# Prompt tiles' output projection and logits: from the merge stage into the samples' attention steps

## The reference

```
mod = silu(c) @ w_ada + b_ada            # sh1, sc1, ga1, sh2, sc2, ga2
h = rms_norm(x, g_pre_mix) * (1 + sc1) + sh1
z = h @ w_in                             # q, k, v, u, s
a = rms_norm(attend(q, k, v, lam), g_subln) * (1 - lam_init)
mix = concatenate([a, s_out]) @ w_out    # 1024 x 1024
x = x + ga1 * rms_norm(mix, g_post_mix)
h2 = rms_norm(x, g_pre_ffn) * (1 + sc2) + sh2
f = hier_moe(h2)                         # 4 + 16 logits a token, top 2 of 16 experts
x = x + ga2 * rms_norm(f, g_post_ffn)
```

## Time and profile before

| | us |
|---|---|
| median of 3 runs | 874.96 (874.81 to 875.82) |
| the profiled execution | 875.83 |
| its span | 874.0 |
| TensorE busy | 764.8 (88%) |
| VectorE busy | 370.9 (42%) |
| ScalarE busy | 166.9 (19%) |
| GpSimd busy | 113.1 (13%) |
| granted TensorE clock, mean | 0.942 |
| DMA, mean over the span | 285 GB/s |

### The profile page before, as it was taken

One profiled execution on the slowest core, in us unless ns is written; L12 is line 12 of the kernel. 1 busy time (PEld: TensorE's weight loads), 2 busy tenths in 40 slices (PEclk: granted clock), 3 DMA queues, 4 the chain that ended last, 5 costly groups with the idle time before them and its releaser, 6 DMA issues. The chain is left out here.

```text
span 874.0 us, 12193 instructions
## 1 busy us (share of the span) xinstructions
PE 764.8 (88%) x5016; PEld 366.6 (42%) x5016; DVE 370.9 (42%) x840; ACT 166.9 (19%) x362; POOL 113.1 (13%) x161
## 2 busy tenths in 40 slices
PE   4699999999998486675779996899999999999994
PEld 3144444444444253333434554444444444444431
DVE  2212262447779897677313667410031011100146
ACT  4001000134455112111201221111011110111132
POOL 2220010200002221121200111000000000000054
PEclk9799999999999898778989997799999999999997
DMA  8988194650004969998989715198889999999792
GB/s 312 393 261 363 35 416 169 225 186 13 13 13 153 382 278 424 429 426 378 372 293 299 320 34 218 49 411 325 333 317 408 421 398 417 401 400 405 305 300 110
DMA packets 37146, 249.26 MB, mean 285 GB/s; under 512 B 4809, under 2 KB 6217, under 8 KB 23650
## 3 DMA queue, kind: packets, MB, share of 16 engines
q1 hardware_dynamic: 23490, 156.35, 45.6%
q0 software_dynamic: 9376, 81.47, 23.9%
q10 hardware_dynamic: 4224, 10.65, 3.6%
HBM read 231.92 MB, written 16.53 MB: 284 GB/s over the span
## 5 line engine op out<-in xcount | busy, mean ns | idle before, releaser
L2351 PE MATMUL ps<-sb 128*128 128x512 f32 (+1 forms) x256 | 112.9, 594 | 0.0
L778 PE MATMUL ps<-sb 128*128 128x512 f32 x192 | 87.1, 609 | 1.4 <-DVE sb L436 1.4
L1429 PE MATMUL ps<-sb 128*32 128x256 f32 x512 | 43.6, 501 | 42.8 <-DMA sb<-in_cache_v,ints 39.3
L2275 DVE TENSOR_TENSOR sb<-sb,ps 128x512 f32<-128x512 f32 (+1 forms) x16 | 10.9, 684 | 160.3 <-PE ps L2351 87.1
L817 DVE STREAM_TRANSPOSE sb<-sb 128x1024 f32<-128x1024 f32 (+1 forms) x72 | 75.8, 1097 | 1.1 <-DMA sb<-in_cache_k,ints 1.1
L2341 PE MATMUL ps<-sb 128*128 128x512 f32 x144 | 66.5, 616 | 1.0 <-ACT sb L2193 0.9
L2376 PE MATMUL ps<-sb 128*128 128x512 f32 x144 | 63.5, 594 | 0.0
L1071 PE MATMUL ps<-sb 128*128 128x512 f32 x128 | 59.2, 598 | 0.3 <-DVE sb L974 0.3
L1997 PE MATMUL ps<-sb 128*128 128x512 f32 x128 | 56.7, 596 | 3.1 <-DVE sb L1693 3.1
L2351 PEld LDWEIGHTS ps<-sb 128*128 128x128 f32 (+1 forms) x256 | 42.1, 167 | 33.9 <-issue 33.9
L778 PEld LDWEIGHTS ps<-sb 128*128 128x128 f32 x192 | 36.5, 195 | 45.7 <-issue 44.4
(11 more groups left out here) (349 smaller groups left out, 962.6 us busy)
## 6 DMA issues: line engine op xcount, KB each, us to landing
sb<-in_w_gate SPq DMA_DIRECT2D x16, 2048.0 KB, 18.8
sb<-in_w_up SPq DMA_DIRECT2D x16, 2048.0 KB, 9.9
sb<-in_w_down SPq DMA_DIRECT2D x16, 2048.0 KB, 14.7
sb<-in_w_ada SPq DMA_DIRECT2D x12, 2048.0 KB, 18.5
sb<-in_w_in SPq DMA_DIRECT2D x5, 2048.0 KB, 24.3
y_rows<-sb SPq DMA_DIRECT2D x9, 512.0 KB, 15.2
sb<-in_w_out SPq DMA_DIRECT2D x2, 2048.0 KB, 25.5
sb<-in_x_prompt SPq DMA_DIRECT2D x4, 512.0 KB, 5.0
```

Source lines behind the costliest of these rows:

```text
L778: last = pe.matmul(PS[:, n % 4, :], L.hT[:, k, t * P:t * P + P], w[:, k, :], start=k == 0, stop=k == KC - 1)
L1429: last = pe.matmul(PS[c:c + 32, 7, 0:256], at[:, page, 32 * quad:32 * quad + 32], vp[:, g, 256 * quad:256 * quad + 256], start=page < 2, s ...
L2351: last = pe.matmul(PS[0:n, 1, :], x[:, k, :], w_up[:, k, :], start=k == 0, stop=k == KC - 1)
```

## The change

The prompt tiles' part of merge moves into attend_sample. TensorE's step b becomes: weights of b - 1, scores of b, values of b - 1, then in odd steps up to 5 the transposes of a tile's mix, in even steps the transposes of a tile's x1, then one half of a tile's projection, and in even steps the logits of that tile. Scores have one buffer instead of two; the first mix tile is turned ahead of the first scores, the first half is projected ahead of the weights of sample 0. ACT does all square sums, all copies of turned tiles, of the weights and of the raw logits, and keeps the first half of a projection in SBUF so that one PSUM bank serves both. x is no longer loaded but added by an accumulating DMA of POOL onto the scaled projection. w_out has a place of its own and is fetched at the start of the stage, the second half after the samples' own scores. Logits of prompt tiles are all made from x1 with scaled router weights. merge keeps tile 3's x1 transposes and logits, h2 of all tiles, the samples' tile, and the routing. Buffers move to other places in SBUF.

The core of the diff, TensorE and POOL in attend_sample:

```diff
+            def rows_of(t):
+                pool.wait_ge(sq1, 2 * t + 2)
...
+                pool.tensor_tensor(ss1[:, t:t + 1], ss1[:, t:t + 1], L.cst("half")[:, 0:1], ALU.pow).then_inc(rs1, 1)
+                pool.wait_ge(scaled, 2 * t + 2)
+                pool.dma_start(x1_of(t), a["x_prompt"][0, t * P:(t + 1) * P, :], accum_op=ALU.add).then_inc(x1_in, 16)
...
+                if b % 2 == 0:
+                    rows_of(b // 2 - 1)
                 if b < SB - 2:
                     keys(b + 2)
...
+            def project_half(u):
+                t, c = u // 2, u % 2
+                pe.wait_ge(mix_ev, 2 * t + 2)
+                pe.wait_ge(wo_in[c], 16)
...
+                for k in range(KC):
+                    last = pe.matmul(PS[:, 5, :], mixT(t)[:, k, :], wo[c][:, k, :], start=k == 0, stop=k == KC - 1)
+                last.then_inc(half_done, 1)
...
+            mix_turn(0, 0)
             pe.wait_ge(q_all, 2)
-            for b in range(SB + 1):
+            scores(0, 0)
+            pe.wait_ge(mix_ev, 2)
+            own_scores()
+            project_half(0)
+            for b in range(1, SB + 1):
                 f, par = b - 1, b % 2
+                for part in range(3):
+                    weights(f, part, 1 - par)
                 if b < SB:
                     scores(b, par)
...
+                values(f)
+                if b < SB:
+                    if b % 2 and b <= 5:
+                        mix_turn((b + 1) // 2, b)
+                    if b % 2 == 0:
+                        x1_turn(b // 2 - 1, b)
+                    project_half(b)
+                    if b % 2 == 0:
+                        logits(b // 2 - 1)
```

SP's fetch of w_out, ACT's rows at the start of the stage, and its new place of the x1 square ahead of exp:

```diff
-            sp.wait_ge(s_done, SB)
+            sp.wait_ge(self.grp_done, 5 * NT)
             for c in range(2):
...
+                if c:
+                    sp.wait_ge(own_done, 1)
+                    sp.wait_ge(self.setup, HP + 1)
+                sp.dma_start(wo[c], a["w_out"][0, :, 512 * c:512 * c + 512].rearrange("(p k) n -> p k n", k=KC)
+                             ).then_inc(wo_in[c], 16)
...
+            act.wait_ge(self.v_out, 16 * NT)
...
+            act.dma_start(x1T, a["g_post_mix"].partition_broadcast(P)).then_inc(rows_in, 16)
+            for f in range(2):
+                c = 2 * D + 512 * f
+                act.dma_start(gate[f], self.mod[NS, c:c + 512].partition_broadcast(P)).then_inc(rows_in, 16)
...
+                    if b and b % 2 == 0:
+                        act.wait_ge(x1_in, 16 * t + 16)
+                        if t:
+                            act.wait_ge(log_done, t)
+                        square(x1T, x1_of(t), ss2[:, t:t + 1], sq2)
                     act.wait_ge(m_ready, b + 1)
```

VectorE at step 0 and merge's new order on SP, ACT and VectorE:

```diff
+                if b == 0:
+                    normed(3)
+                    dve.wait_ge(rows_in, 96)
+                    for f in range(2):
+                        last = dve.tensor_tensor(gate[f], gate[f], x1T[:, 512 * f:512 * f + 512], ALU.mult)
...
+            sp.wait_ge(self.sample["pv"], SB - 1)
+            for kind in range(2):
+                self.load_expert(sp, 0, 0, kind)
             sp.wait_ge(self.sample["pv"], SB)
+            self.load_expert(sp, 0, 0, 2)
+            self.load_expert(sp, 1, 1, 0)
+            for i in range(2):
+                sp.wait_ge(h2_out2[i], (48, 32)[i])
             self.load_expert(sp, 1, 1, 1)
             self.load_expert(sp, 1, 1, 2)
...
+            store(1)
+            keep_logits(3)
+            store(2)
+            act.wait_ge(mix_tr, 5)
+            act.activation(mixT, PS[:, 6, :].rearrange("p (k t) -> p k t", k=KC), ACT.Copy).then_inc(mix_ev, 1)
+            store(3)
+            act.wait_ge(summed, 2)
+            square(hv[4][0:NS], proj, ss1[0:NS, 4:5], sq1)
...
+            dve.wait_ge(rows_in, 96 + 16 * 8)
...
+            h2_of(0, scale2, shift2)
+            self.last_sum(SB - 1, 1)
+            h2_of(1, scale2, shift2)
...
+            dve.wait_ge(o_in, 16 * SB)
+            self.head_norm(dve, link, osb, sq, ss8, L.mix[0:NS, 4, 0:512], NS, ss_ready, ss_power, 1
+                           ).then_inc(mix_ready, 1)
             route(0, 3)
+            h2_of(2, scale2, shift2)
+            for c in range(2):
+                dve.wait_ge(half_done, 9 + c)
...
+            h2_of(3, scale2, shift2)
+            dve.wait_ge(rs1, 5)
```

More of the change, by code:

```diff
@@ L1250, in _ @@
[L1250 to L1251 removed]
+                values(b)
+                if b == SB - 2:
+                    pool.wait_ge(s_done, SB - 1)
+                    for half in range(2):
+                        self.load_pages(pool, self.cv, SB - 1, half, LAST_V_SLOT[half])
+                if b % 2 and b >= 3:
+                    t = (b - 3) // 2
+                    pool.wait_ge(sq2, t + 1)
+                    self.power(pool, link, ss2[:, t:t + 1], 1, P, 1.0 / D, rs2)
@@ L1678, in _ @@
+            square(hv[4][0:NS], self.x1[0:NS, 4, :], ss2[0:NS, 4:5], sq2)
+            act.wait_ge(x1_tr, 5)
+            act.activation(h2T, PS[:, 6, :].rearrange("p (k t) -> p k t", k=KC), ACT.Copy).then_inc(x1_ev, 1)
+            store(4)
             act.wait_ge(exp_in, 1)
@@ new lines, in _ @@
+            x1_turn(3, SB)
+            logits(3)
+            pe.wait_ge(mix_ready, 1)
+            pe.wait_ge(self.sample["at_act"], 3 * SB)
+            for k in range(KC):
+                last = pe.transpose(PS[:, 6, NS * k:NS * k + NS], L.mix[0:NS, 4, k::KC], L.cst("ident", NS)[:, 0:NS])
+            last.then_inc(mix_tr, 1)
+            pe.wait_ge(mix_ev, 9)
+            pe.wait_ge(x1_ev, 8)
+            for c in range(2):
+                for k in range(KC // 2):
+                    for c0, kk in ((0, k), (NS, k + KC // 2)):
+                        last = pe.matmul(PS[c0:c0 + NS, 2 + c, :], mixT[:, kk, :], tile["wo"][c][:, kk, :],
+                                         start=k == 0, stop=k == KC // 2 - 1)
+                last.then_inc(half_done, 1)
```

717 lines of the change are left out of this document (305 added, 412 removed).

## The result

The changed kernel takes 909.89 us (median of 4, 907.99 to 912.81), the kernel before 874.88: a ratio of 1.040, interval 1.037 to 1.043. The profiled execution took 909.85 (span 908.0). The forecast was 881, range 862 to 896. The sign was right and the size was not: +34 on the profiled execution where the sum said +6.4.

A forecast was written before the change was run, and what follows sets the result against it. The samples' stretch was taken as bound by its transfers, merge as part matmul, part latency. +21.6 up to the last values and -15.2 in merge gave +6.4 on 875.8, so 882, median 881; range 862 to 896.

The forecast's parts named there:

- E: End of the last sample's values, 447.0 us in the kernel before; forecast to move by +21.6 to 468.6.
- Start: Up to sample 0's end: TensorE waits for w_out's first half, landing at 312; +10.6 us (bounds +2, +15).
- Middle: Samples 1 to 5: TensorE's work stays just under the transfers' time, key gathers issued before queues run dry; +2.6 us.
- Rival (b): Accumulating x transfer is slow, exp and key gathers late in even steps; +14, 894 us; 0.17 shared with late merge.
- The forecast's own alarm: Sign set beforehand: forecast wrong if ACT or TensorE stand for x1 over 2 us per even step.
- Sample 6: Step without key fetches, 13.5 us before: TensorE alone now needs 20.5; +6.9 us (bounds +5, +8).
- firmest term: The forecast's words for its sample 6 term, +6.9 us.
- Sample 7: Last sample: expert 0's first weights share the queues with the last values; +1.5 us (bounds -0.5, +4).
- Merge: From the last sample's values to the first expert gate: 90 us against 105.2, so -15.2 (bounds 80 to 98).
- Behind the first gate: Experts and combine, 322 us as before: nothing changes.
- (a): Both w_out and merge's rows come early: start +3, merge 83; 865 us; chance 0.28.
- (c): A wash: steps at their lower bound, merge as forecast, +13 - 14, 874 us; chance 0.12.

The follow-up runs named there:

- b2: Changed kernel with projection half 0 moved behind scores 1 and VectorE's gate products behind step 0; 897.44 us, ratio 1.024.
- a4: Changed kernel with both w_out transfers cut to 64 columns and the product left out; total not usable, four samples 92.2 us.
- f3: Kernel before with eight idle matmuls (7.0 us) ahead of scores 2 to 7, nothing else of the change; 880.70 us, ratio 1.004.
- f4: Kernel before with eight idle matmuls (7.0 us) behind scores 2 to 7, nothing else of the change; 877.06 us, ratio 1.001.
- b1_order: Changed kernel with TensorE's projection half moved between a step's scores and its values, from step 1 on; 907.07 us, ratio 1.035.
- d3_order_xadd: Changed kernel: projection halves and transposes ahead of values, half 0 behind scores 1, gates behind step 0, plain x transfer added by VectorE; 888.37 us.
- a2: Changed kernel with x's rows fetched by a plain transfer, the sum left out; total not usable, four samples 91.5 us.
- a3: Changed kernel with the accumulating x transfer cut to 16 of 1024 columns; total not usable, four samples 90.7 us.
- b4: Changed kernel with x's rows fetched by a plain transfer on SyncE's queue and added by VectorE; 909.81 us, ratio 1.041.
- b3: Changed kernel with merge's eight row transfers issued early, in the last but one step; 908.64 us, ratio 1.037.
- d1: Changed kernel with the experts' first weights held until merge's eight row transfers have landed; 914.45 us, ratio 1.047.
- g1: Changed kernel with the experts' first weights held until merge's rows and the last o fetch have landed; 902.07 us, ratio 1.028.
- g2: d3_order_xadd with merge's rows issued behind the last sample's exp and the experts' weights held behind rows and o fetches; 867.08 us, ratio 0.989.

## Why the prediction was right or wrong

E was forecast at +21.6 and came at +47.1. By step:

**Start: +10.6 forecast, +18.2 measured.** w_out's first half landed at 317.7, not 312, and the half behind it took 9.11 us, not 6.9: TensorE had stood 18.9 us before it, and the granted clock was 0.50 from 300 to 320 us, the lower level. 5.7 + 2.2 = 7.9 is the whole miss of 7.6. For the landing I had taken a value between the bounds "with less ahead of it". The nearest row (23.2 us) would have given 316. The Trainium skill ("DMA: Bandwidth & Descriptors", section on queues, rings and completion order), read as in the forecast, gave 315 to 316, nearer than mine but still early: measured 24.8 us from issue to landing. Whether the packets are the reason, no run here shows. b2 shows the price of the order: with half 0 behind scores 1 sample 0 ends 7.4 us earlier. VectorE's wait was nearly as long: the rows let it go at 316.6, not at about 310, and in a4, with w_out cut, the weights of sample 0 still started only at 320.1 (326.8 in the changed kernel), behind VectorE's coefficients.

**Middle: +2.6 forecast, +21.1 measured.** This is the step that failed, and the sentence in it is "the gathers of the next keys are issued 1 to 3 us before the queue runs dry". In every second step they were issued after it had run dry (share 0.04 from 380 to 382), and TensorE, for which no wait was forecast, stood for values: 5.3 us in sample 1 (25.9 us, forecast 20.0) and 10.2 us in the next four (94.1, forecast 81.8). f3 and f4 show that the projection half alone is nearly as cheap as forecast. What I had not followed is the change of order that comes with it: weights now stand ahead of the scores, and so do transposes, the half and logits. The chain from a sample's end to the next keys' issue grew from some 5 to 14.8 us in one step and 17.1 to 17.9 in the next. The sum of TensorE's work was right in the even steps (21.0 measured, 20.5 forecast) and too small in the odd ones, 20.2 and 21.1 for 18.7: after the waits the values' last part ran at the lower level (granted clock 0.50 from 408 to 410) and took 2.83 + 1.07 us, where the forecast had 1.87 + 0.55. Delay of the keys against four samples:

| kernel | keys issued after the sample's end | four samples | TensorE's waits for values in them |
|---|---|---|---|
| before | 4.7 to 5.2 | 79.9 | 25.7 |
| f3_ahead7 | 11.7 | 81.3 | none |
| b1_order | 7.9 and 12.8 to 14.7 | 87.0 | none over 0.6 |
| d3_order_xadd | 6.8 and 9.9 to 10.3 | 82.9 | none |
| after | 14.8 and 17.1 to 17.9 | 94.1 | 10.2 |

The delay is no law by itself: the kernel before is bound by its transfers, f3, b1 and d3 by TensorE's own step, and only the changed kernel pays for both. Of its 14.2 us in four samples 10.2 are waits for values, the rest is TensorE's own time over 79.9. Clear of noise is that one moved line (b1) takes these waits away and 7.1 us with them. The half alone costs 1.4 (f3) and the accumulating transfer with its bytes 2 to 3 (a2, a3), both within noise or hardly over it. From b1 to d3 another 4.1 go, of them 3.4 are b1's waits for the copy of x1. That x1's chain only comes free once the order has been mended is argued from b4, which gained nothing alone; no run adds b4 to b1 alone. The shares overlap and are not sums of independent parts.

Rival (b) named the right transfer for a part of it. It put 3 to 4 us on each; the queue lost 1.5 to 2. The forecast's own alarm, "if ACT stands for x1 over 2 us per even step", went off: 13.4 us each time. The wait was not hidden, since exp came late, but by b4 it was not the last to arrive.

**Sample 6: +6.9 forecast, +9.0 measured.** TensorE stood 1.0 us in the scores and their matmuls were slower than the sum had them (4.41 + 1.05). The "firmest term" was 2 short. **Sample 7: +1.5 forecast, -1.1 measured.** The experts' weights did not hold up the last values: TensorE's only wait in it is 0.69 us, for ScalarE.

**Merge: 90 forecast, 93.0 measured.** Right in size and order: rows at +24.2 for +21, head norm at +36.5 (its second instruction is at 531.27) for +34.1, the copy behind the third h2 store, the samples' projection 8.59 for 9.5. b3, d1 and g1 show what the rows wait for: I had priced them by a store under load, and it is the 8.4 MB of weights in the same queues (+24.2 with them, +17.2 without, d1). In the kernel before SyncE waits for merge's transfers before it loads the first expert (its lines `sp.wait_ge(mod_in, 16 * 5)` and the five on x), and the change drops that wait. I had that fact in front of me, as "no weights in the way", and did not list it as something that the change removes. Keeping that wait alone would have been no gain: d1 does it, and its total is 4.6 us longer, since the weights then meet the o fetch. In the kernel before the o fetches are issued at 465.0 to 467.8, ahead of the weights (469.8). Holding the weights behind both is worth 7.8 us (g1).

**Behind the first gate: nothing**, 320.9 against 321.8. Right.

Rivals (a) and (c) are out; (b) was the nearest, at 894 still 16 us short. (c) writes merge as -14, where the forecast's sum has -15.2; nothing hangs on it. That the sign came out right is in part luck: it rested on the start and sample 6, which were forecast as losses and were larger ones, while the largest term stood at almost nothing. The error behind that term: I took TensorE's step and the transfers' step as a maximum (18.7 or 20.5 against 19.8), where slots that are freed late make them partly a sum.

## What to carry to other kernels

Where a step's transfers wait for buffers that the step's matmuls free, follow the chain from the end of one step to the next issue, not only the totals. Seven us of matmuls ahead of the freeing instruction cost 1.4 us in four steps (f3, not clear of noise); with weights, transposes and logits ahead of it as well, and x's chain beside it, the same matmuls cost 14.2. Put added work behind the instruction that frees a buffer where you can: one line moved so gave 7 us in four steps (b1). When several waits end close together, mend them together before judging any: here single repairs gave +2.6, -0.1 and -12.5 us and the three together -21.5.

## What the runs showed of the hardware

An accumulating transfer holds the DMA engines longer than its bytes: share 0.99 at 263 GB/s around it, 426 GB/s around the same transfer without accumulation (a2). The shortfall of 0.65 MB in 4 us is more than the transfer's own 0.5 MB, so the gathers beside it slow down as well.

Seven transfers of 16 KB took ScalarE 10.56 us to issue behind eight row transfers and beside the experts' weights, and 16.12 us in b3. Where the weights were held they took 2.75 us (d1), 3.03 (g1) and 2.45 (g2), in d1 and g1 behind the same eight row transfers. So issuing can cost time while other transfers are under way; what it waits for, no run shows.

TensorE has more room under a transfer bound than its busy time says. The kernel before and f4_beside7, the same 20 us (columns as above):

```profile
340.00:360.00 20.00, 12.88 (x229) 6.54 (x197) 13.36 (x24) 2.96 (x4) 3.43 (x4) 0.74 1.00 424
```

```profile
340.00:360.00 20.00, 19.00 (x302) 10.68 (x298) 15.24 (x28) 3.23 (x5) 5.13 (x6) 1.00 1.01 430
```

With 7 us of work added per step TensorE was granted full speed (1.00) where it had been granted 0.74, a mean over its two levels, and the queues moved as many bytes in the same time. Before, it stood for values in every step (39.3 us in all) and ran at the lower level in part; the slower matmuls had been filling its waits.
